# Picking the first expert pair's rows with TensorE products, the table products of three tiles ahead of the last tile's ranks

## The reference

```python
g_logits = t @ wg + bg                     # 4 groups, t = rms_norm(h) * norm_ffn
group = argmax(g_logits)
e_sel = (t @ we + be)[group's 8 experts]
top_val, top_idx = top_k(e_sel, 2)
gate = one_hot(group) x softmax(top_val) * p_group
y = sum over the 32 experts of  gate * (silu(t @ w1[e]) * (t @ w3[e])) @ w2[e]
h = h + y
```

## Time and profile before

| | |
|---|---|
| runs shown, median of 3 | 1679.25 us (1678.71, 1679.25, 1692.91) |
| profiled execution, its own time | 1684.34 us |
| span of the profiled execution | 1682.5 us |
| mean granted TensorE clock | 0.966 |
| TensorE matmul busy | 1522.7 us, 91% |
| VectorE busy | 802.8 us, 48% |
| ScalarE busy | 419.4 us, 25% |
| GpSimd busy | 162.1 us, 10% |
| DMA moved | 315.04 MB, mean 187 GB/s |
| chain that ended last | TensorE 72%, DMA 14%, VectorE 5%, ScalarE 3%, issue 3% |

### The profile page before, as it was taken

How to read it: one execution, slowest core, us unless ns; L and a number is a source line. 1 busy time by engine, 2 the same in 40 slices (tenths; PEclk the granted TensorE clock), 3 DMA queues, 4 the chain that set the end, 5 groups by cost and what they waited for, 6 DMA issues and landing times.

```text
span 1682.5 us, 29007 instructions
## 1 busy us (share of the span) xinstructions
PE 1522.7 (91%) x12509; PEld 934.8 (56%) x12509; DVE 802.8 (48%) x1403; ACT 419.4 (25%) x849; POOL 162.1 (10%) x183
## 2 busy tenths in 40 slices
PE   6999998889999999699887899999999997988886
PEld 4786777777644864433332378746558545333232
DVE  7655555553754445543221356446643544432125
ACT  2124255454301131400000120027421323000002
POOL 2000223231000000011111200000000001111001
PEclk9999999999999999799999999999999997999898
DMA  8208200011541521579999922220034234999995
GB/s 277 100 1 287 82 4 5 4 48 35 200 150 50 200 100 54 206 295 424 424 425 425 352 84 100 100 100 1 1 128 176 99 114 155 396 425 424 425 407 203
DMA packets 82338, 315.04 MB, mean 187 GB/s; under 512 B 17968, under 2 KB 19048, under 8 KB 57312
## 3 DMA queue, kind: packets, MB, share of 16 engines
q1 hardware_dynamic: 70112, 284.86, 43.6%
q0 software_dynamic: 10944, 24.10, 3.9%
q10 hardware_dynamic: 1152, 4.19, 0.6%
HBM read 306.86 MB, written 34.34 MB: 203 GB/s over the span
## 4 chain that ended last, share of the span: by engine, by line
PE 72%; DMA 14%; DVE 5%; ACT 3%; issue 3%; SPq 2%; PEld 0%; ACTq 0%; DVEq 0%; POOLq 0%
PE PS L790 20%; PE PS L657 13%; DMA arena<-in_moe_w 11%; PE PS L1442 9%; PE PS L2743 7%; PE PS L2768 5%; PE PS L1836 2%; PE PS L1772 2%; PE PS L2692 2%; PE PS L628 2%; PE PS L1812 1%; DMA ring<-in_moe_w 1%; PE PS L2097 1%; PE PS L2118 1%; PE PS L552 1%
## 5 line engine op out<-in xcount | busy, mean ns | idle before, releaser
L790 PE MATMUL PS<-arena,ring 128*128 128x256 f32 x1344 | 299.5, 383 | 2.8 <-DVE arena L934 2.8
L790 PEld LDWEIGHTS PS<-arena,ring 128*128 128x128 f32 x1344 | 255.6, 192 | 42.3 <-issue 6.3
L2743 PE MATMUL PS<-arena 128*64 128x512 f32 x704 | 166.4, 628 | 24.9 <-DMA arena<-in_moe_w 24.9
L657 PE MATMUL PS<-ring,arena 128*128 128x512 f32 x400 | 179.9, 596 | 0.7 <-ACT arena L2063 0.7
L2743 PEld LDWEIGHTS PS<-arena 128*64 128x64 f32 x704 | 52.6, 144 | 136.2 <-issue 103.3
L657 PEld LDWEIGHTS PS<-ring,arena 128*128 128x128 f32 x400 | 74.6, 192 | 83.3 <-issue 82.3
L2751 DVE TENSOR_TENSOR arena<-PS,arena 128x256 f32<-128x256 f32 x32 | 13.6, 424 | 218.6 <-PE PS L2758 201.3
L2748 ACT ACTIVATE arena<-PS 128x256 f32<-128x256 f32 x32 | 12.3, 383 | 327.7 <-PE PS L2743 327.7
L2743 PE MATMUL PS<-ring,arena 128*64 128x512 f32 x320 | 77.0, 637 | 16.1 <-DMA ring<-in_moe_w 12.9
L839 DVE TENSOR_TENSOR arena<-arena,PS 128x512 f32<-128x512 f32 x56 | 36.8, 684 | 112.4 <-PE PS L790 112.4
L1442 PE MATMUL PS<-ring 64*64 64x64 f32 (+1 forms) x3072 | 77.4, 234 | 10.6 <-issue 9.4
(11 more groups left out here) (336 smaller groups left out, 2219.0 us busy)
## 6 DMA issues: line engine op xcount, KB each, us to landing
arena<-in_moe_w SPq DMA_DIRECT2D x120, 1024.0 KB, 20.0
ring<-in_moe_w SPq DMA_DIRECT2D x72, 1024.0 KB, 17.6
ring<-in_sb_wqkv SPq DMA_DIRECT2D x6, 2048.0 KB, 9.2
ring<-in_xa_wq SPq DMA_DIRECT2D x4, 2048.0 KB, 8.6
ring<-in_xa_wo SPq DMA_DIRECT2D x4, 2048.0 KB, 14.2
ring<-in_xa_wkv SPq DMA_DIRECT2D x3, 2048.0 KB, 10.3
h<-in_x SPq DMA_DIRECT2D x8, 512.0 KB, 8.9
ring<-in_rw_wr SPq DMA_DIRECT2D x2, 2048.0 KB, 11.4
```

The costliest lines, as they stand in the source:

```text
L657: ins = pe.matmul(PS[:, BANK_OF[g], :], rows(k), cols[:, k, :], start=(k == 0 and not grows), stop=(k == 3), skip_group_check=grows)
L790: ins = pe.matmul(PS[:, BANK_OF[g], M * c:M * c + M], rows[:, k, o:o + P], cols[:, k, :], start=(c + k == 0 and not grows), stop=(k == 3), ...
L2743: ins = pe.matmul(bank(2, 2, F)[r, :, :], xgT[p][:, k, r], w[a][:, :, k, :], start=(k == 0), stop=(k == KC - 1))
```

## The change

- GpSimd (`pick_rows`) and, for the last tile, VectorE (in `place(3)`) build for every tile a matrix `picks` of 128 tokens by 128 slots: at (token, slot) it holds the token's 1/rms if the token goes to that slot of pair 0, else 0. GpSimd does it for tiles 0, 1, 2: per tile one 128x2, two 128x128 tensor_scalar and one 128x128 tensor_tensor. Tile 3 takes one 128x2, two 128x128 and one 128x128 on VectorE.
- TensorE (`pick_tile`) multiplies `h` by `picks`, eight products of 128x128 per tile, summed over the four tiles in PSUM banks 0 and 3. The result is what the gather and the eight turns of pair 0 gave. Tile 0's products stand ahead of the turning of tile 3, those of tiles 1 and 2 right behind `route_logits(3)`, then the tables of tiles 0 to 2, then `route_ranks(3)`, then tile 3's picks in two halves.
- The gather of pair 0 and its turns are gone; the two `nop`s that free `xg` no longer wait for the table.
- Tile 3's table product, the counts (`rest_of_table_pe`) stand between the halves of up(0). So the table and the gather of pair 1 come after up(0)'s first half.
- On VectorE `place(1)` stands ahead of `second(2)`. In `moe_route_vec` the scaling into `xgT` comes first, `gdiff` and `ed` next, the table behind them.
- On GpSimd the picks of tile 0 stand ahead of the two memsets of `xg`, those of tiles 1 and 2 behind them, and all of them ahead of the first gather.

```diff
@@ cross_pe: end of the output product
+            pick_tile(pe, l, 0)
             late_turn(pe, ffn, NT - 1, ready, range(3))
             route_logits(pe, l, NT - 1, ahead)
@@
+        def pick_tile(pe, l, t, ks=range(KC)):
+            if t < NT - 1:
+                pe.wait_ge(S("first_picks"), 14 * l + (4, 10, 14)[t])
+            else:
+                pe.wait_ge(S("first_rows"), 3 * l + 1)
+            for k in ks:
+                ins = pe.matmul(bank(PICK_BANKS[k // 4], 4, P)[:, k % 4, :], h[:, t, k::KC], picks[t % 3][:, 0, :],
+                                start=(t == 0 and k % 4 == 0), stop=True, ...)
+            return ins
         def moe_route_pe(pe, l):
+            pick_tile(pe, l, 1)
+            pick_tile(pe, l, 2)
             for t in range(NT - 1):
-                filled_table(t)
+                filled_table(pe, l, t)
             route_ranks(pe, l, NT - 1)
-            filled_table(NT - 1).then_inc(S("tabled"), 1)
+            pick_tile(pe, l, NT - 1, range(KC // 2)).then_inc(S("first_rows"), 1)
+            for p in range(2):
+                pe.nop().then_inc(S(f"xg_free{p}"), 1)
+            pick_tile(pe, l, NT - 1, range(KC // 2, KC)).then_inc(S("xg_free0"), 1)
+
+        def rest_of_table_pe(pe, l):
+            filled_table(pe, l, NT - 1).then_inc(S("tabled"), 1)
             pe.wait_ge(S("chosen"), 2 * NT * (l + 1))
             scores_read(pe, l, 8)
             pe.matmul(PS[:, 4, 384:384 + NE], ones[:, :], cum[:, NT, :], ...)
@@ place(t)
+                if t == NT - 1:
+                    own = picks[t % 3]
+                    for k in range(2):
+                        do(vec.tensor_scalar(own[:, k, :], iob, s8[...], w_pick[:, k, t:t + 1], ALU.is_equal, ALU.mult))
+                    vec.tensor_tensor(own[:, 0, :], own[:, 0, :], own[:, 1, :], ALU.add).then_inc(S("first_rows"), 1)
@@ moe_choice_vec
+            place(1)
             second(2)
-            place(1)
             place(2)
             scale(3)
             group_and_first(3)
             second(3)
+            vec.wait_ge(S("onehots"), 28 * l + 10)
+            do(vec.tensor_scalar(w_pick[:, :, NT - 1], OB[:, NT - 1, :, 0], rstd[:, NT - 1:NT], None, ALU.mult))
             place(3)
@@ moe_route_vec
+            vec.wait_ge(S("first_rows"), 3 * l + 2)
+            xgT_first(vec, l, 0).then_inc(S("first_rows"), 1)
+            vec.wait_ge(S("xg_free0"), (NPE // 2 + 1) * l + 2)
+            xgT_first(vec, l, 1).then_inc(S("xgT_ready"), 1)
@@ moe_pool
+            def pick_rows(t, before):
+                b, own = 14 * l + before, picks[t]
+                pool.wait_ge(S("onehots"), 28 * l + (4, 6, 9)[t])
+                pool.tensor_scalar(w_pick[:, :, t], OB[:, t, :, 0], rstd[:, t:t + 1], None, ALU.mult)...
+                for k in range(2):
+                    pool.tensor_scalar(own[:, k, :], iob, s8[...], w_pick[:, k, t:t + 1], ALU.is_equal, ALU.mult)...
+                pool.tensor_tensor(own[:, 0, :], own[:, 0, :], own[:, 1, :], ALU.add).then_inc(S("first_picks"), 1)
+            pick_rows(0, 0)
             (memsets of xg)
+            pick_rows(1, 6)
+            pick_rows(2, 10)
...
-            for n in range(4):
+            for n in range(1, 4):
                 fetch(n)
@@ moe_pe, up_pair(n)
                 if n == 0:
-                    pe.wait_ge(S("first_rows"), 2 * l + 2)
+                    pe.wait_ge(S("first_rows"), 3 * l + 3)
                     up(pe, p, 2, w, range(KC // 2))
+                    rest_of_table_pe(pe, l)
                 pe.wait_ge(S("xgT_ready"), NPE * l + n + 1)
                 up(pe, p, 2, w, range(KC // 2 if n == 0 else 0, KC)).then_inc(S("up_done"), 1)
@@ moe_pe
-            pe.wait_ge(S("table_ready"), l + 1)
-            for p in range(2):
-                pe.nop().then_inc(S(f"xg_free{p}"), 1)
-            turn(0)
             for n in range(NPE):
```

More of the change, by code:

```diff
@@ L1863, in trunk @@
         XO_SUMS = at(20, [4, 512]), at(15, [4, 2 * P])
+        PICK_BANKS = (0, 3)
         def cross_act(act, l, before):
@@ L2169, in trunk @@
         hidT = at(27.5, [2, P])
+        picks = [at(27, [2, P]), at(27.5, [2, P]), at(26, [2, P])]
         yg = [at(12 + n, [C]) for n in range(8)]
@@ L2300, in route_ranks, with filled_table @@
             pe.matmul(v, ones[:, :], cum[:, t, :], start=False, stop=True).then_inc(S("ranked"), 1)
-        def moe_route_pe(pe, l):
[L2303 to L2308, removed]
+        def pick_tile(pe, l, t, ks=range(KC)):
[5 more added lines that the diff above has]
+                ins = pe.matmul(bank(PICK_BANKS[k // 4], 4, P)[:, k % 4, :], h[:, t, k::KC], picks[t % 3][:, 0, :],
+                                start=(t == 0 and k % 4 == 0), stop=True,
+                                skip_group_check=not (t == 0 and k % 4 == 0))
+            return ins
+        def filled_table(pe, l, t):
+            pe.wait_ge(S("onehots"), 28 * l + (4, 6, 9, 12)[t])
+            for k in range(2):
+                ins = pe.matmul(PS[:, 5, 0:NPE], OS[:, t, k, :], OB[:, t, k, :], start=(t + k == 0),
+                                stop=(t + k == NT))
+            return ins
+        def moe_route_pe(pe, l):
+            pick_tile(pe, l, 1)
+            pick_tile(pe, l, 2)
             for t in range(NT - 1):
-                filled_table(t)
+                filled_table(pe, l, t)
             route_ranks(pe, l, NT - 1)
-            filled_table(NT - 1).then_inc(S("tabled"), 1)
+            pick_tile(pe, l, NT - 1, range(KC // 2)).then_inc(S("first_rows"), 1)
[4 more added lines that the diff above has]
+            filled_table(pe, l, NT - 1).then_inc(S("tabled"), 1)
             pe.wait_ge(S("chosen"), 2 * NT * (l + 1))
@@ L2467, in moe_route_vec @@
             do = stepper(vec, l)
+            vec.wait_ge(S("first_rows"), 3 * l + 2)
+            xgT_first(vec, l, 0).then_inc(S("first_rows"), 1)
+            vec.wait_ge(S("xg_free0"), (NPE // 2 + 1) * l + 2)
+            xgT_first(vec, l, 1).then_inc(S("xgT_ready"), 1)
+            vec.tensor_tensor(gdiff, lg[:, :, 0:G], gmax.unsqueeze(2).to_broadcast([P, NT, G]), ALU.subtract)\
+                .then_inc(S("route_a"), 1)
+            vec.tensor_tensor(ed, v2, v1, ALU.subtract).then_inc(S("route_a"), 1)
             vec.wait_ge(S("tabled"), 9 * l + 1)
@@ L2637, in fetch @@
                 gather(pool, p, P, table[:, n:n + 1]).then_inc(S(f"xg_in{p}"), 16)
+            def pick_rows(t, before):
+                b, own = 14 * l + before, picks[t]
+                pool.wait_ge(S("onehots"), 28 * l + (4, 6, 9)[t])
+                pool.tensor_scalar(w_pick[:, :, t], OB[:, t, :, 0], rstd[:, t:t + 1], None, ALU.mult)\
+                    .then_inc(S("first_picks"), 1)
+                pool.wait_ge(S("first_picks"), b + 1)
+                for k in range(2):
+                    m = NT * k + t
+                    pool.tensor_scalar(own[:, k, :], iob, s8[:, m:m + 1], w_pick[:, k, t:t + 1], ALU.is_equal, ALU.mult)\
+                        .then_inc(S("first_picks"), 1)
+                pool.wait_ge(S("first_picks"), b + 3)
+                pool.tensor_tensor(own[:, 0, :], own[:, 0, :], own[:, 1, :], ALU.add).then_inc(S("first_picks"), 1)
+            pick_rows(0, 0)
             pool.wait_ge(S("proj_filled"), FIRST[f"xo{l}"] + 14)
             for p in range(2):
-                pool.memset(xg[p], 0.0).then_inc(S("xg_cleared"), 1)
-            pool.wait_ge(S("xg_cleared"), 2 * l + 2)
+                pool.memset(xg[p], 0.0).then_inc(S("first_picks"), 1)
+            pick_rows(1, 6)
+            pick_rows(2, 10)
+            pool.wait_ge(S("first_picks"), 14 * l + 14)
             for t in range(2):
@@ L2724, in spread_out, with xgT_first @@
             vec.tensor_copy(gatesT[p].rearrange("p t s -> p (t s)"), PS[:, 3, :]).then_inc(S("gates_last"), 1)
+        def xgT_first(vec, l, b):
+            return vec.tensor_tensor(xgT[0][:, 4 * b:4 * b + 4, :], bank(PICK_BANKS[b], 4, P)[:, :, :],
+                                     gainT[:, GAIN[f"ffn{l}"], 4 * b:4 * b + 4].unsqueeze(2)
+                                     .to_broadcast([P, 4, P]), ALU.mult)
         def turn_rows(pe, p, rows, ks=range(KC)):
@@ L2785, in turn @@
             def turn(n):
[L2786 to L2791, removed]
+                pe.wait_ge(S(f"xg_in{n % 2}"), 16 * ((NPE // 2 - 1 + n % 2) * l + (n + 1) // 2))
+                turn_rows(pe, n % 2, P).then_inc(S(f"xg_free{n % 2}"), 1)
             def up_pair(n):
@@ L2860, in turned @@
             def turned(n):
-                if n == 0:
-                    vec.wait_ge(S("first_rows"), 2 * l + 1)
-                    xgT_out(vec, l, 0, P, (0,)).then_inc(S("first_rows"), 1)
                 vec.wait_ge(S(f"xg_free{n % 2}"), (NPE // 2 + 1) * l + n // 2 + 2)
-                xgT_out(vec, l, n % 2, P, (1,) if n == 0 else range(2)).then_inc(S("xgT_ready"), 1)
+                xgT_out(vec, l, n % 2, P).then_inc(S("xgT_ready"), 1)
             def rows(n):
```

7 lines of the change are left out of this document (3 added, 4 removed).

## The result

The changed kernel takes **1692.63 us** (median of 20 runs, 1686.42 to 1699.49), the kernel before beside it 1681.45. The ratio is 1.0062, 95% interval 1.0047 to 1.0077: 10.4 us slower (7.9 to 12.9; the two medians lie 11.2 apart), where I had forecast 4 faster, and outside the range. The profiled execution has its own time at 1695.66 us, a span of 1693.9 and a mean granted clock of 0.968, against 1684.34, 1682.5 and 0.966.

The account below looks back on a forecast made before the run. Experts bound by the weight stream, held back until up(0) ends. Earlier up(0) less a 1.2 us hole gains 2.6 and 1.5 us, together 4.1: 1684.34 to 1680.2, as a median 1675; range 1664 to 1685.

Parts of the forecast that it names:

- a 128-wide record at full clock is 0.89/8 = 0.111 us: Unit cost for the pick products on TensorE; a tile's 16 records take 1.8 us full, 3.7 half.
- the middle term: Picks of tiles 1 and 2 and tables ahead of the last ranks: 6.7 us; 4.85 at full clock, 9.9 at half.
- My own price for half clock there, 5.5: Ranks to up(0) at half clock, with ranks 1.0 and picks 1.84; at full clock 4.1 us.
- case A: Clock back amid the picks, half clock for their first 3.65 us, then full: 1675; chance 0.42.
- B: Full clock throughout, tile 0's picks filling the idle hole: gain of 13.9 us together, 1665; chance 0.20.
- rule on turns: A transpose does not count as busy for the clock, so tile 3's turns starve it; the sum stays mixed.
- So the turns of pair 1 wait some 1.2 us: Pair 1's gather starts amid up(0), so its turns wait, leaving a stream hole of about 1.2 us per layer.
- C: Clock does not come back for the 128-wide picks: loss of 7.1 us together, 1686; chance 0.15.
- D: Pair 1's gather lands late beside the weight stream: 1.5 us per layer, 1678; chance 0.13.
- E: TensorE waits for GpSimd's picks of tile 2: costs 2.5 and 1.4 us at the long end, 1679; chance 0.10.
- `place(1)` ahead of `second(2)`: On VectorE, puts 1.1 us ahead of tile 2's choice; costed at nothing, bounded by 1.1.
- what counts is when up(0) ends: Every us earlier moves 210 us of weight stream and all behind it; the end follows, less the hole.

Follow-up runs that it names:

- e1: The changed kernel with pick products reading h in one contiguous piece instead of every eighth feature; ratio 1.0001 to the kernel before.
- e8: The changed kernel with each pick product replaced by two turns (transposes) of the same step-8 piece of h; ratio 0.9996 to the kernel before.
- e3: The changed kernel with tile 3's table product and the counts in front of up(0) instead of between its halves; ratio 1.0019 to the kernel before.
- e2: The changed kernel with steps of 1, 2, 4 and 8 in the reads of h for tiles 0 to 3; one execution, 1687.18 us.
- e4: The changed kernel with the tables of tiles 1 and 2 moved back amid up(0), in front of tile 3's; 1687.20 us, ratio 1.0048 to the kernel before.
- e5: The changed kernel with picks stationary and h moving, 512 wide, then copies and eight turns, last table early; ratio 0.9971 to the kernel before.
- e6: The changed kernel with the edits of e1 and e3 together: contiguous h and early last table; 1678.52 us, ratio 0.9961 to the kernel before.
- e7: e5 with the tables of tiles 0 to 2 ahead of tile 2's picks; 1673.14 us, ratio 0.9942 to the kernel before.

## Why the prediction was wrong

My steps against what was measured, us, layer 0 / layer 1:

| step | predicted | measured |
|---|---|---|
| tile 1's ranks to tile 3's turns (tile 0's picks stand here) | 3.2 / 2.3 | 4.3 / 4.3 |
| turns and scores of tile 3 | 4.9 / 4.8 | 3.6 / 3.6 |
| picks of tiles 1 and 2, tables | 6.7 / 6.7 | 9.0 / 9.0 |
| last ranks to up(0) | 4.1 / 4.1 | 6.5 / 6.5 |
| up(0) with the table | 10.0 / 9.8 | 9.1 / 8.8 |
| gap to the next load, over before's 9.8 | 1.2 / 1.2 | 4.8 / 4.2 |
| sum | 30.1 / 28.9 | 37.3 / 36.3 |

**The first step that failed is "a 128-wide record at full clock is 0.89/8 = 0.111 us"**, the unit cost behind "32 x 0.111" and behind "1.8 us full". The row is of products with a contiguous stationary operand; the picks load `h[:, t, k::KC]`, step 8. Measured at full clock: 0.244. It stands in three rows of the table: tile 0's picks take 4.1 us and no longer fit into the idle stretch, the middle term takes 2.3 us more than forecast though the clock was full, and a part of the fourth row. In that row tile 3's 16 records take 4.19 us where I had 0.9 for half of them before the scaling, but they ran at half clock, where contiguous ones take 3.58 (e1, layer 1) and the whole row 5.9 us in place of 6.5; e8 has 5.7 and 5.8. So only 0.6 to 0.8 of the 2.4 us over the forecast go with the step, and the rest with the slow clock. My own price for half clock there, 5.5, left out that the second half of the picks (1.84) lasts longer than the scaling (1.0) that it was to hide behind. e1 and e8 each take the step's price away: their stretches are 4.7 to 6.2 us shorter than the change's in each layer.

**The assumption on the clock failed too, and hid the first error's size.** I took case A, half clock for the first 3.65 us of the picks. In fact B's condition held up to the last ranks: 1.00 from the turns of tile 3 to 712.2. By B's own sum (4.85 us) the middle term would have been missed by 4.1 us, not 2.3. From 713.9 to some 720 the clock was down, where my sum had tile 3's picks at full clock, so B as a whole ("full clock throughout") did not come true either. What B got right is the row of turns and scores, some 1.2 us under my sum in each layer. The Trainium skill's rule on turns that I weighed (they don't count as busy, so tile 3's turns starve the clock) did not show in the change: through them the clock stood at 1.00 (the first window above), behind tile 0's dense picks, and in e8, where 32 more turns follow, it still did. It is not refuted: in e3's layer 1 the clock fell right behind tile 3's turns and scores. What had stood in the picks' place before, and is gone, is 2.68 and 1.46 us of idling.

**The second step that failed is "So the turns of pair 1 wait some 1.2 us ... and the stream gets a hole of about that".** The mechanism was right and the wait near: 2.2 and 1.4 us. What I left out is what the wait does to the clock. I named its fall after idling as the mark of the stretch before up(0), and then priced up(1), behind a wait and eight turns, at full clock. It took 9.72 and 9.92 us instead of 7.09, so 2.6 and 2.8 of the 4.8 and 4.2 are clock. It does not fall every time. Up(1) was slow (8.4 to 9.9 us) behind waits for the gather of 1.44 to 2.21 us, in the change, e1's layer 0, e2's layer 0 and e4's layer 1, and took 7.09 behind waits of 1.36 to 1.69, in e4's layer 0, e1's and e2's layer 1 and both of e8. So the length of the wait does not tell the cases apart, and what does is open; e3 shows that without the wait the term is gone.

**The rivals.** C gave a loss, and 1686, by half clock through the picks; the 32 picks on which it hung were slow at full clock, so its sign was right and its mechanism wrong. D asked for a gather later by 1.5 us: it took 4.68 us from issue to landing (724.65 to 729.33), against 3.62 and 4.10, which is part of the longer wait in layer 0. E did not occur in the change: GpSimd takes 2.5 us a tile, two 128x128 steps of 0.80 and one of 0.45, and was done at 705.7 where TensorE came by at 706.5. It does occur once picks are quick (e1, e5, e6, e8: 1.1 to 1.2 us).

**Terms that held.** `place(1)` ahead of `second(2)` moved nothing: VectorE's choice of tile 3 was ready at 708.0 and then VectorE idled 4.32 us for the ranks. VectorE beside GpSimd's picks was slowed to 0.32 us for a step that otherwise takes 0.23, far less than the 0.79 of the memset. And "what counts is when up(0) ends, and the end follows by as much less the hole" held for the change: 10.3 by the two layers, 10.4 at the end, with the luck named above; for the quicker kernels the end followed by 3 to 7 us less.

## What to carry to other kernels

Before taking a duration from a row of the same shape, compare the access pattern of **each** operand, the stationary one first, and the mode: a turn with the same step is no witness for a product. If the stationary operand would be strided, swap the two sides, even at the price of a copy and of turns (e5's 0.9971 against e3's 1.0019, both with the table early); laying out `xgT` and the weights so that the strided read becomes contiguous was not tried. Read the clock beside every unit cost: the step doubles a record's time at full clock and hardly shows at half. And where a change puts a wait and turns ahead of a long product, price that product at the slow clock as well as the fast one.

## What the runs showed of the hardware

- At full clock the load of a stationary 128x128 float32 operand of a product takes 0.192 us contiguous (e1), 0.196 with a step of 2, 0.325 to 0.329 with 4 (e2), 0.336 with 8 (the change); in series a record every 0.12 or every 0.24 us. A turn with a step of 8 loads in 0.188 to 0.195.
- At half clock the stride costs little: the contiguous load takes 0.333 us (e1, layer 1, 1407.3 to 1409.9) and the strided one 0.338 (the change, 714.4 to 717.5), both with the clock at 0.50; by the starts of these 13 and 14 loads that is a record every 0.22 against every 0.24 us. Tile 3's 16 picks took 4.19 us strided in the change and 3.58 contiguous in e1's layer 1, where the clock was 0.69 in their first half us; at full clock 4.07 and 2.03. The strided load hardly follows TensorE's clock, and the 32 picks took 7.89 us in the change at 1.00 and in e3's layer 1, where it began at 0.50. The turn's load does not double either: 0.231 us at half clock (e8, layer 1).
- Four records of 128x512 take 1.96 us, sixteen contiguous ones of 128x128 2.03, for one tile's picks at full clock (e5, e1).
- The clock was at 0.50 amid tile 3's picks, behind TensorE's wait of 1.73 us for VectorE, in the change and in every experiment but e7, in both layers (in e2's layer 1 it had fallen before). In e7 it stayed at 1.00, behind the same 1.73. What differed ahead of it was a wait of 1.1 us for GpSimd in e5, filled in e7; in the change and in e3 there was no such wait, so what decides is open.
